# Loading the second expert of each pair through the scalar engine's DMA queue

## The chip, the cores and the metric

The kernel runs on one core of a Trainium2 chip. The core has a matmul engine (TensorE, PE in the profile, with its weight loads shown apart as PEld), a vector engine (DVE), a scalar engine (ACT), GpSimd (POOL) and a sync engine (SP) that computes nothing and only issues DMA transfers. All transfers run on the same 16 DMA engines; a transfer is put on the queue of the engine that issues it. The metric is the device time of one execution in microseconds. The figure for a kernel is the median over several runs.

## The reference: what is computed

Two transformer blocks over 256 tokens of width 1024, everything in fp32, batch 1. The first block mixes (a spatial gating unit and attention), then has an MLP of width 4096 and a gated projection. The second has a state-space and attention mixer and ends in a mixture of experts, which is the part that matters here:

```python
t = h.reshape(-1, d)                       # 256 tokens x 1024
g_sel = argmax(t @ w_router_group)         # 1 group of 8
top_logit, top_local = top_k(in_group, 2)  # 2 experts of the 8 in that group
# for each of the 64 experts e, on the tokens that chose it:
hid = silu(xb @ w_gate[e]) * (xb @ w_up[e])    # 1024 -> 512
y   = hid @ w_down[e]                          # 512 -> 1024, times the token's gate, added up
```

There are 64 experts. Each has three matrices of 1024 x 512 fp32 (gate, up, down), 2 MB each, so the weights of the experts are 64 x 3 x 2 MB. Each token uses two experts, so an expert sees few tokens, and one that no token chose need not be loaded.

## The kernel before

The program is written engine by engine: each engine has its own instruction list, and semaphores order them. A semaphore is named after what it counts: `gated`, `upped` and `downed` count the pairs whose gate, up and down matmuls are done; `pair_landed[...]` counts landed weights.

**The first 700 us** (both mixers, the MLP) stream 1 MB weight panels through three raw buffers. The change doesn't touch them.

**The experts.** The 64 experts are taken in 32 pairs; two pairs make a couple. `experts(couple, odd, ...)` exists once for PE, once for ACT and once for DVE, and each handles pair `i = 2 * couple + odd`. PE's steps for a pair:

1. gate matmuls (line 1132, 32 matmuls), reading both experts' gate panels, then `gated` goes up
2. up matmuls (also line 1132, 32 matmuls), then `upped` goes up
3. small work: in odd pairs the gather of the next couple's tokens (L1102), in both the scatter of the pair before (L1112), and two turns (transposes, L1146 and L1150)
4. down matmuls (L1168, 32 matmuls), then `downed` goes up

Before each of the three big steps PE waits for the weights of both experts, e = 0 and e = 1:

```python
for e in range(2):
    pe.wait_ge(pair_landed["down", e], 16 * (i + 1))
```

ACT's steps for a pair: silu of the gate result after `gated` (L722), a copy of the turned hidden values (L726), a sum over the gates (L730), and after `downed` a scaled copy of both halves of the result (L736). In odd pairs it also copies gathered tokens (L716).

**Buffers.** Up and down have one buffer for each of e = 0 and 1; gate has two, for even pairs in the tile `slots` and for odd pairs in the tile `areas`. So gate of pair i + 2 can be loaded once gate of pair i has been used, but up and down of pair i + 1 only when those of pair i have been used.

**Loading.** SP issues all the loads, one instruction of 2 MB for each expert and matrix (L376). After the first pair (and gate of pair 1) its fixed order is up(i), gate(i+1), down(i), up(i+1), ..., each time e = 0 and then e = 1. Each step first reads the two token counts from `count_i` (L380), then waits until the buffer was used, and issues the loads with a condition: an expert with zero tokens is not moved, though its semaphore is still counted up. SP works strictly in this order, so gate(i+1) is issued behind up(i) even where its buffer came free earlier. A second pass over all experts, for experts with over 64 tokens, is in the program but is not entered with these inputs.

Of the kernel before, what the change touches and what calls it, by code (L numbers as in the profile page):

```python
# [26 lines left out]
P = 128  # L27
D = 1024
S = 256
# [13 lines left out]
SLOTS = 64  # L43
PAIRS = NE // 2
# [44 lines left out]
def program(nc, x_in, p_in, norm_mix_g, w_in, w_sgu, b_sgu, ln_v_g, ln_v_b, rel_bias, w_out, norm_ffn_g,  # L89
# [24 lines left out]
    with ExitStack() as ctx:  # L114
        def sb(name, shape, dt=F32):
            return ctx.enter_context(nc.sbuf_tensor(name, shape, dt))
# [51 lines left out]
        count_i = sb("count_i", [P, NE + 1], I32)  # L168
# [154 lines left out]
        @block.sync  # L323
        def _(sp):
            sp.dma_start(x[:, :, :], x_in[0].rearrange("(m p) c -> p m c", p=P)).then_inc(x_loaded, 16)
            def load_rows():
                sources = {"norm_mix_g": norm_mix_g, "norm_ffn_g": norm_ffn_g, "norm_ple_g": norm_ple_g, "b_sgu": b_sgu,
                           "norm_mix_2": norm_mix_2, "conv_w": conv_w, "conv_b": conv_b, "ssd_norm": ssd_norm,
                           "attn_norm": attn_norm, "norm_ffn_2": norm_ffn_2}
                for name, (first, n) in ROWS.items():  # L330
                    src = sources[name]
                    if name == "conv_w":
                        src = src[0].rearrange("j (c p) -> (j c) p", p=P)
                    elif name == "b_sgu":
                        src = src[0]
                    else:
                        src = src[0].rearrange("(c p) -> c p", p=P)
                    sp.dma_start(small_rows[first:first + n], src).then_inc(rows_loaded, 16)

            for q in range(2 * NP):  # L340
                p, (kind, j) = q // 2, PANELS[q // 2]
                k = shape(p)[0] // 2
                if q >= RAW:
                    sp.wait_ge(w_ready, q - RAW + 1)
                sp.dma_start(loaded(q),
                             panel_source(kind, j)[:, k * (q % 2):k * (q % 2) + k, :]).then_inc(landed[q % RAW], 16)
                if q == 0:
                    load_rows()
                if q == 1:
                    sp.dma_start(table[0:BUCKETS, :], rel_bias).then_inc(table_loaded, 16)  # L350
                    sp.dma_start(area(6)[0:BUCKETS + 1, 0:LINE], bucket_of_line).then_inc(bucket_loaded, 16)
                    sp.dma_start(w_s, w_sgu[0].rearrange("g t s -> t g s")).then_inc(ws_loaded, 16)
                if q == 3:
                    sp.dma_start(ln_vecs[:, 0, :], ln_v_g.to_broadcast([P, D])).then_inc(ln_loaded, 16)
                    sp.dma_start(ln_vecs[:, 1, :], ln_v_b.to_broadcast([P, D])).then_inc(ln_loaded, 16)
                if q == 11:
                    for n, v in enumerate((dt_bias, a_log, d_skip, attn_sinks)):
                        sp.dma_start(heads4[:, n, :], v.to_broadcast([P, HEADS])).then_inc(heads_loaded, 16)
                    sp.dma_start(dtw[:, :, :], columns(w_in_2, 2560, HEADS)).then_inc(dtw_loaded, 16)


            def load(w, i, pair, odd, beyond):
                weights, used = {"gate": (w_gate, gated), "up": (w_up, upped), "down": (w_down, downed)}[w]


                tokens = [None if beyond is None else tokens_of(pair, e) for e in range(2)]
                if isinstance(i, int) and i == 0:
                    sp.wait_ge(panel_done, NP)
                elif isinstance(i, int) and w == "gate":
                    sp.wait_ge(t_made, MT)  # L370
                    sp.wait_ge(routed, 1)
                else:
                    sp.wait_ge(used, i - 1 if w == "gate" else i)
                for e in range(2):
                    cond = {} if beyond is None else {"cond": tokens[e] > beyond}
                    sp.dma_start(expert_panel(w, e, odd), weights[0, 2 * pair + e].rearrange("(p k) n -> p k n", p=P),  # L376
                                 **cond).then_inc(pair_landed["odd_gate" if w == "gate" and odd else w, e], 16)

            def tokens_of(pair, e):
                return sp.value_load(count_i[0:1, bass.ds(2 * pair + e, 1)], min_val=0, max_val=S)  # L380

            def rest_of_pass(first, beyond):

                with sp.Fori(0, PAIRS // 2 - 1) as j:
                    for n in (1, 2):
                        for w, ahead in (("up", 0), ("gate", 1), ("down", 0)):
                            load(w, 2 * j + n + ahead + first, 2 * j + n + ahead, (n + ahead) % 2, beyond)
                for w in ("up", "down"):
                    load(w, first + PAIRS - 1, PAIRS - 1, 1, beyond)

            for w in ("gate", "up", "down"):
                load(w, 0, 0, 0, None)
            load("gate", 1, 1, 1, None)
            sp.wait_ge(marks_done, 1)
            fullest = sp.value_load(count_i[0:1, NE:NE + 1], min_val=0, max_val=S)
            rest_of_pass(0, 0)
            with sp.If(fullest > SLOTS):
                with sp.Fori(1, PASSES) as r:
                    for w in ("gate", "up", "down"):
                        load(w, r * PAIRS, 0, 0, r * SLOTS)  # L400
                    load("gate", r * PAIRS + 1, 1, 1, r * SLOTS)
                    rest_of_pass(r * PAIRS, r * SLOTS)
            for m in range(MT):
                sp.wait_ge(out_ready, m + 1)
                sp.dma_start(out[0, P * m:P * m + P, :], xn[:, m, :]).then_inc(out_stored, 16)
            sp.wait_ge(out_stored, 16 * MT)
# [61 lines left out]
        def _(act):  # L468
# [244 lines left out]
            def gather(couple, half):  # L713

                act.wait_ge(gathered, 4 * couple + 2 * half + 1)
                act_(xeT[:, 4 * half:4 * half + 2].rearrange("p k o s -> p (k o s)"), banks[0][:, :], ACT.Copy).then_inc(xe_a, 1)  # L716

            def experts(couple, odd, first=False, last=False):

                i = 2 * couple + odd  # L720
                act.wait_ge(gated, i + 1)
                act_(h_e[:, :], banks[2][:, :], ACT.Silu).then_inc(silu_ready, 1)  # L722
                if odd and not last:
                    gather(couple + 1, 0)
                act.wait_ge(he_turned, i + 1)
                act_(heT[:, :, :].rearrange("p c s -> p (c s)"), banks[2][:, :], ACT.Copy).then_inc(heT_ready, 1)  # L726
                act.wait_ge(put_turned, i + 1)
                if not first:
                    act.wait_ge(ye_d, i)
                act_(gates_seen[:, :], banks[3][:, 0:S], ACT.Copy, accum_out=gate_of_slot).then_inc(gate_kept, 1)  # L730
                if odd and not last:
                    gather(couple + 1, 1)
                act.wait_ge(gate_kept, i + 1)
                act.wait_ge(downed, i + 1)
                for half in range(2):
                    act_(y_hi[:, 512 * half:512 * half + 512], banks[half][:, :], ACT.Copy, scale=gate_of_slot).then_inc(ye_a, 1)  # L736

            gather(0, 0)
            gather(0, 1)
            experts(0, 0, first=True)  # L740
            experts(0, 1)
            fullest = act.value_load(count_i[0:1, NE:NE + 1], min_val=0, max_val=S)
            with act.Fori(1, PAIRS // 2 - 1) as j:
                experts(j, 0)
                experts(j, 1)
            experts(PAIRS // 2 - 1, 0)
            experts(PAIRS // 2 - 1, 1, last=True)
            with act.If(fullest > SLOTS):
                with act.Fori(1, PASSES) as r:
                    gather(r * (PAIRS // 2), 0)  # L750
                    gather(r * (PAIRS // 2), 1)
                    with act.Fori(0, PAIRS // 2 - 1) as j:
                        experts(r * (PAIRS // 2) + j, 0)
                        experts(r * (PAIRS // 2) + j, 1)
                    experts(r * (PAIRS // 2) + (PAIRS // 2 - 1), 0)
                    experts(r * (PAIRS // 2) + (PAIRS // 2 - 1), 1, last=True)
            load_roots()
            act.wait_ge(x_ready, X_MOE)
            sum_squares(x, D, xn)
# [1041 lines left out]
```

## Time and profile before

| | |
|---|---|
| runs (3): median, lowest, highest | 1677.53, 1676.45, 1678.44 us |
| profiled execution: its own time | 1678.98 us |
| its span, first to last instruction | 1677.2 us |
| PE busy | 1508.0 us, 90% |
| DVE, ACT busy | 577.1 us (34%), 452.3 us (27%) |
| moved by DMA | 489.21 MB, mean 292 GB/s |
| queues: SP's (hardware) and GpSimd's (software) | 484.17 MB and 4.26 MB |

The span is the stretch that the trace shows; the time of the same execution is 1.8 us longer. The page cuts the span into 40 slices of 41.9 us; experts run from slice 18 on (about 717 us) to the end. A busy PE in this profile need not be PE at its peak. "SPq" and "ACTq" are instructions that an engine's sequencer handles itself, such as the issue of a transfer.

### The profile page before, as it was taken

What the parts mean: (1) busy time and instruction counts of PE and PEld (TensorE: products, weight loads), DVE (VectorE), ACT (ScalarE), POOL (GpSimd) and SP (SyncE); (2) the same over time, 40 slices, a digit from 0 to 9 for tenths busy, and PEclk for the clock granted to TensorE, in tenths of its full rate; (3) what the DMA queues carried; (4) which work ended last, traced back from release to release, by engine and by line L of the source; (5) the groups of instructions that cost most, each with busy time, mean ns of one, the idle gap of its engine ahead of it and who ended that gap; (6) DMA issues with size and microseconds to landing.
All of it is one profiled execution on the core that took longest, in us unless ns stands there. A gap on an engine that the chain in (4) does not pass through costs nothing.

```text
span 1677.2 us, 20152 instructions
## 1 busy us (share of the span) xinstructions
PE 1508.0 (90%) x7961; PEld 959.4 (57%) x7963; DVE 577.1 (34%) x934; ACT 452.3 (27%) x720; POOL 25.9 (2%) x34
## 2 busy tenths in 40 slices
PE   7999979999979988959999889888988989999976
PEld 5897869988769977744344334434433443444432
DVE  5745655644554897541111011111101111111102
ACT  5435645543444464321011011111101111111101
POOL 1000000000000000020000000000000000000000
PEclk9999989999979997979999999999999999999998
DMA  8463344455333331287999999999999999998993
GB/s 291 157 236 113 122 147 149 162 193 188 135 119 120 105 121 68 57 368 308 404 389 428 429 428 429 428 429 428 429 427 429 428 429 395 416 428 370 429 408 127
DMA packets 80269, 489.21 MB, mean 292 GB/s; under 512 B 6423, under 2 KB 8595, under 8 KB 56788
## 3 DMA queue, kind: packets, MB, share of 16 engines
q1 hardware_dynamic: 79028, 484.17, 71.3%
q0 software_dynamic: 1184, 4.26, 0.8%
q8 instruction: 39, 0.64, 0.2%
q14 instruction: 18, 0.15, 0.0%
HBM read 506.20 MB, written 1.08 MB: 302 GB/s over the span
## 4 chain that ended last, share of the span: by engine, by line
PE 54%; DMA 20%; DVE 7%; issue 2%; ACT 2%; SPq 1%; DVEq 0%; ACTq 0%
DMA slots<-in_w_down_dram 20%; PE bank L796 19%; PE bank L1168 15%; PE bank L1132 12%; PE bank L1102 3%; PE bank L1112 2%; DVE w_lo L1267 1%; SPq L376 1%; DVE h_lo L1257 1%; PE bank L779 1%; DVE areas L1517 1%; PE bank L1053 1%; DVE xeT L1701 1%; PE bank L1043 0%; DVE areas L1220 0%
## 5 line engine op out<-in xcount | busy, mean ns | idle before, releaser
L1132 PE MATMUL bank<-slots,xeT 128*64 128x512 f32 x1536 | 335.4, 592 | 0.8 <-issue 0.8
L1168 PE MATMUL bank<-slots,heT 128*64 128x512 f32 x1024 | 250.1, 645 | 65.5 <-DMA slots<-in_w_down_dram 64.0
L1132 PEld LDWEIGHTS bank<-slots,xeT 128*64 128x64 f32 x1536 | 118.7, 137 | 211.2 <-issue 211.2
L1267 DVE TENSOR_TENSOR w_lo<-raw,w_hi 128x2048 fp32r<-128x2048 f32 (+2 forms) x98 | 208.9, 2166 | 75.6 <-ACT w_hi L522 75.4
L1168 PEld LDWEIGHTS bank<-slots,heT 128*64 128x64 f32 x1024 | 82.6, 148 | 214.6 <-issue 211.5
L522 ACT ACTIVATE w_hi<-raw 128x2048 fp32r<-128x2048 f32 (+2 forms) x98 | 173.6, 1816 | 62.1 <-PE bank L796 56.6
L796 PE MATMUL bank<-h_hi,w_hi 128*128 128x256 f32 x560 | 160.8, 287 | 0.2 <-DVE h_lo L1257 0.2
L796 PE MATMUL bank<-h_lo,w_hi 128*128 128x256 f32 x560 | 159.1, 284 | 0.0
L796 PE MATMUL bank<-h_hi,w_lo 128*128 128x256 f32 x560 | 159.1, 284 | 0.0
L1723 DVE SCALAR_TENSOR_TENSOR y_lo<-bank,stats,y_hi 128x512 fp32r<-128x512 f32 x64 | 45.1, 746 | 313.1 <-ACT y_hi L736 313.1
L1710 DVE TENSOR_TENSOR h_e<-bank,h_e 128x512 f32<-128x512 f32 x32 | 22.1, 692 | 363.7 <-PE bank L1132 363.7
L796 PE MATMUL bank<-w_hi,h_hi 128*128 128x512 f32 (+1 forms) x344 | 138.1, 402 | 7.9 <-DVE h_lo L1257 3.0
L796 PE MATMUL bank<-w_hi,h_lo 128*128 128x512 f32 (+1 forms) x344 | 134.1, 390 | 0.0
L796 PE MATMUL bank<-w_lo,h_hi 128*128 128x512 f32 (+1 forms) x344 | 133.9, 389 | 0.0
L736 ACT ACTIVATE y_hi<-bank,stats 128x512 fp32r<-128x512 f32 x64 | 40.5, 684 | 339.1 <-PE bank L1168 339.1
L1132 PE MATMUL bank<-areas,xeT 128*64 128x512 f32 x512 | 112.8, 592 | 0.0
L796 PEld LDWEIGHTS bank<-h_hi,w_hi 128*128 128x128 f32 x560 | 108.2, 193 | 2.1 <-issue 0.6
L796 PEld LDWEIGHTS bank<-h_lo,w_hi 128*128 128x128 f32 x560 | 108.2, 193 | 0.0
L796 PEld LDWEIGHTS bank<-h_hi,w_lo 128*128 128x128 f32 x560 | 108.1, 193 | 0.0
L1132 PEld LDWEIGHTS bank<-areas,xeT 128*64 128x64 f32 x512 | 40.3, 137 | 69.6 <-issue 69.6
L796 PEld LDWEIGHTS bank<-w_hi,h_hi 128*128 128x128 f32 x344 | 66.0, 192 | 24.5 <-issue 7.2
L796 PEld LDWEIGHTS bank<-w_hi,h_lo 128*128 128x128 f32 x344 | 65.6, 191 | 13.8
(301 smaller groups left out, 1637.5 us busy)
## 6 DMA issues: line engine op xcount, KB each, us to landing
slots<-in_w_up_dram SPq DMA_DIRECT2D x64, 2048.0 KB, 15.4
slots<-in_w_down_dram SPq DMA_DIRECT2D x64, 2048.0 KB, 19.3
slots<-in_w_gate_dram SPq DMA_DIRECT2D x32, 2048.0 KB, 19.3
areas<-in_w_gate_dram SPq DMA_DIRECT2D x32, 2048.0 KB, 21.8
raw<-in_w_in_dram SPq DMA_DIRECT2D x42, 1024.0 KB, 6.2
raw<-in_w_ff_dram SPq DMA_DIRECT2D x32, 1024.0 KB, 5.3
raw<-in_w_out_dram SPq DMA_DIRECT2D x12, 1024.0 KB, 5.1
raw<-in_w_ple_gate_dram SPq DMA_DIRECT2D x4, 1024.0 KB, 5.6
```

The lines of the kernel that those rows point to most:

```text
L376: sp.dma_start(expert_panel(w, e, odd), weights[0, 2 * pair + e].rearrange("(p k) n -> p k n", p=P), **cond).then_inc(pair_landed["odd_gat ...
L522: last = act_(hi, source, ACT.Copy)
L736: act_(y_hi[:, 512 * half:512 * half + 512], banks[half][:, :], ACT.Copy, scale=gate_of_slot).then_inc(ye_a, 1)
L779: last = turn_tile(banks[b][:, at:at + P], src[:, m, P * k:P * k + P], ident[:, :])
L796: last = mm(psum, a[i][a_at], b[j][b_at], start=(start and n == 0), stop=(stop and n == 2))
L1102: last = mm(banks[b][:, S * (k % 2):S * (k % 2) + S], t[:, m, P * k:P * k + P], pick_r[:, m, :, :].rearrange("p e s -> p (e s)"), start=(m ...
L1112: last = mm(banks[4 + 2 * m + half][:, :], put[:, m, :], y[:, 512 * half:512 * half + 512], start=False, stop=False)
L1132: last = mm(bank[SLOTS * e:SLOTS * e + SLOTS, :], xeT[:, k, odd, SLOTS * e:SLOTS * e + SLOTS], expert_panel(w, e, odd)[:, k, :], start=(k ...
L1168: last = mm(banks[half][SLOTS * e:SLOTS * e + SLOTS, :], heT[:, c, SLOTS * e:SLOTS * e + SLOTS], expert_panel("down", e, odd)[:, c, 512 * ...
L1267: last = tt(lo, source, hi, ALU.subtract)
L1710: tt(h_e[:, :], banks[3][:, :], h_e[:, :], ALU.mult).then_inc(he_ready, 1)
L1723: last_part = stt(y_lo[:, 512 * half:512 * half + 512], banks[half][:, :], gate_of_slot, y_hi[:, 512 * half:512 * half + 512].bitcast(F32) ...
```

## The change

From pair 1's up on (and gate from pair 2 on), SP issues only the load of e = 0. The load of e = 1 is issued by ACT, through ACT's own DMA queue, by a new function `load_second` that ACT calls at three places of its `experts`: gate of pair i + 2 behind the silu of pair i, up of pair i + 1 after the gates' sum (in odd pairs after the second token copy too), and down of pair i + 1 behind the two scaled copies of pair i. No new semaphore wait is added there, as ACT has already waited for what shows the buffer to be free. What is read, its sizes, buffers and conditions stay. PE's and DVE's programs stay as they are.

```diff
-            def load(w, i, pair, odd, beyond):
+            def load(w, i, pair, odd, beyond, both=True):
...
-                for e in range(2):
+                for e in range(2 if both else 1):
...
                         for w, ahead in (("up", 0), ("gate", 1), ("down", 0)):
-                            load(w, 2 * j + n + ahead + first, 2 * j + n + ahead, (n + ahead) % 2, beyond)
+                            load(w, 2 * j + n + ahead + first, 2 * j + n + ahead, (n + ahead) % 2, beyond, both=False)
...
+            def load_second(w, pair, odd, beyond):
+
+                weights = {"gate": w_gate, "up": w_up, "down": w_down}[w]
+                tokens = act.value_load(count_i[0:1, bass.ds(2 * pair + 1, 1)], min_val=0, max_val=S)
+                act.dma_start(expert_panel(w, 1, odd), weights[0, 2 * pair + 1].rearrange("(p k) n -> p k n", p=P),
+                              cond=tokens > beyond).then_inc(pair_landed["odd_gate" if w == "gate" and odd else w, 1], 16)
+
-            def experts(couple, odd, first=False, last=False):
+            def experts(couple, odd, in_pass, beyond, first=False, last=False):
...
                 act.wait_ge(gated, i + 1)
                 act_(h_e[:, :], banks[2][:, :], ACT.Silu).then_inc(silu_ready, 1)
+                if not last:
+                    load_second("gate", 2 * in_pass + odd + 2, odd, beyond)
                 if odd and not last:
                     gather(couple + 1, 0)
...
                 if odd and not last:
                     gather(couple + 1, 1)
+                if not (odd and last):
+                    load_second("up", 2 * in_pass + odd + 1, 1 - odd, beyond)
                 act.wait_ge(gate_kept, i + 1)
                 act.wait_ge(downed, i + 1)
                 for half in range(2):
                     act_(y_hi[:, 512 * half:512 * half + 512], banks[half][:, :], ACT.Copy, scale=gate_of_slot).then_inc(ye_a, 1)
+                if not (odd and last):
+                    load_second("down", 2 * in_pass + odd + 1, 1 - odd, beyond)
```

Where the instructions stand: ACT's program of one even pair in the loop over couples, before (`h_e` is the silu, `heT` the turned copy, `gates_seen` the gates' sum, `y_hi` the scaled copies).

```order
L722 ACTIVATE h_e<-bank 128x512 [waits gated]
L726 ACTIVATE heT<-bank 128x512 [waits he_turned]
L730 ACTIVATE gates_seen,stats<-bank 128x256 [waits ye_by_vector,put_turned]
L736 ACTIVATE y_hi<-bank,stats 128x512 [waits downed,gate_kept]
L736 ACTIVATE y_hi<-bank,stats 128x512
```

The first and the last part of the same pair in the changed kernel (the up load, left out here, stands between them in the same way; "ISA" rows are register work).

```order
L729 ACTIVATE h_e<-bank 128x512 [waits gated]
L721 ISA
L721 TENSOR_LOAD count_i
L721 ISA x2
L722 ISA
L722 DMA slots<-in_w_gate_dram 128x4096
L735 ACTIVATE heT<-bank 128x512 [waits he_turned]
...
L747 ACTIVATE y_hi<-bank,stats 128x512 [waits downed,gate_kept]
L747 ACTIVATE y_hi<-bank,stats 128x512
L721 TENSOR_LOAD count_i
L721 ISA x2
L722 ISA
L722 DMA slots<-in_w_down_dram 128x4096
```

Three loads of e = 1 have moved into ACT's program, each behind work of ACT and with no wait of its own.

SP's program at up and gate in the same loop, as before:

```order
L376 ISA [waits upped]
L376 DMA slots<-in_w_up_dram 128x4096
L376 ISA
L376 DMA slots<-in_w_up_dram 128x4096
...
L376 ISA [waits gated]
L376 DMA slots<-in_w_gate_dram 128x4096
L376 ISA
L376 DMA slots<-in_w_gate_dram 128x4096
```

And in the changed kernel:

```order
L376 ISA [waits upped]
L376 DMA slots<-in_w_up_dram 128x4096
...
L376 ISA [waits gated]
L376 DMA slots<-in_w_gate_dram 128x4096
```

SP still takes up before gate, with one load each; the gate load of e = 1 no longer stands behind SP's wait for `upped`.

## Rows read from the trace of the kernel before

**Rows 1.** The page: slices of the span, and queues.
```profile
DMA  8463344455333331287999999999999999998993
GB/s 291 157 236 113 122 147 149 162 193 188 135 119 120 105 121 68 57 368 308 404 389 428 429 428 429 428 429 428 429 427 429 428 429 395 416 428 370 429 408 127
...
q1 hardware_dynamic: 79028, 484.17, 71.3%
q0 software_dynamic: 1184, 4.26, 0.8%
```

**Rows 2.** Waits over the whole span: us in total, times, longest us.
```profile
ACT y_hi L736 <- PE bank L1168: 339.1, 32, 15.3
...
ACT h_e L722 <- PE bank L1132: 178.7, 32, 7.0
ACT heT L726 <- PE bank L1146: 160.3, 32, 8.8
...
PE bank L1168 <- DMA slots<-in_w_down_dram: 64.0, 17, 6.6
```

**Rows 3.** Stretches: us, engines' busy time (instructions), TensorE clock, DMA share, GB/s.
```profile
758.00:770.00 12.00, 11.01 (x54) 4.51 (x50) 0.69 (x1) 0.92 (x2) 0.00 (x0) 1.00 0.11 27
823.00:827.00 4.00, 3.69 (x20) 2.30 (x16) 0.69 (x1) 0.49 (x1) 0.00 (x0) 1.00 0.62 184
845.00:851.00 6.00, 5.83 (x37) 3.43 (x33) 1.38 (x2) 0.99 (x2) 0.00 (x0) 1.00 0.41 137
1422.00:1427.00 5.00, 5.00 (x31) 2.96 (x28) 0.69 (x1) 0.60 (x1) 0.00 (x0) 1.00 0.37 102
1509.00:1513.00 4.00, 3.53 (x20) 2.43 (x18) 0.69 (x1) 0.86 (x3) 0.00 (x0) 1.00 0.73 246
1531.00:1536.00 5.00, 5.00 (x34) 3.05 (x31) 0.94 (x2) 0.60 (x1) 0.00 (x0) 1.00 0.36 95
1633.00:1637.00 4.00, 4.00 (x22) 1.47 (x20) 0.86 (x2) 1.27 (x2) 0.00 (x0) 1.00 0.38 94
851.00:1422.00 571.00, 523.36 (x2486) 229.65 (x2488) 74.89 (x118) 67.47 (x139) 0.00 (x0) 0.96 1.01 428
```

**Rows 4.** Timeline at one gap of pair 23: start us, length us, what.
```profile
1417.91 7.07 PE L1132 MATMUL bank<-slots,xeT 128*64 128x512 f32 x32
1418.15 0.60 ACT L722 ACTIVATE h_e<-bank 128x512 f32<-128x512 f32 x1 [5.54 <-PE bank L1132]
...
1425.29 0.97 SPq L376 DMA_DIRECT2D slots<-in_w_up_dram  x2
```

**Rows 5.** Timeline at the first gap, pair 0, and the next PE wait.
```profile
754.09 13.95 PE L1132 MATMUL bank<-slots,xeT 128*64 128x512 f32 x64 [0.83 <-issue]
...
768.38 1.02 SPq L376 DMA_DIRECT2D slots<-in_w_up_dram  x2
...
801.80 8.42 PE L1168 MATMUL bank<-slots,heT 128*64 128x512 f32 x32 [3.69 <-DMA slots<-in_w_down_dram]
```

**Rows 6.** Stretches at the end of the first gap, columns as above.
```profile
768.50:769.00 0.50, 0.10 (x1) 0.11 (x2) 0.34 (x1) 0.00 (x0) 0.00 (x0) 1.00 0.00 0
769.00:769.50 0.50, 0.50 (x5) 0.50 (x6) 0.00 (x0) 0.00 (x0) 0.00 (x0) 1.00 1.50 328
```

**Rows 7.** SP's loads (L376, L380): duration ns min/median/max.
```profile
L380 SPq TENSOR_LOAD <-count_i x184: 261/268/283, 746.8 to 1618.3; - x184
...
L376 SPq FUSED_REGOPS  x184: 149/174/200, 768.1 to 1635.9; - x184
L376 SPq DMA_DIRECT2D slots<-in_w_up_dram x64: 88/333/532, 718.2 to 1617.4; - x64
```

**Rows 8.** Timeline of the last two pairs.
```profile
1603.16 1.00 SPq L376 DMA_DIRECT2D slots<-in_w_down_dram  x2
...
1625.85 9.40 PE L1168 MATMUL bank<-slots,heT 128*64 128x512 f32 x32 [6.61 <-DMA slots<-in_w_down_dram]
...
1652.65 7.09 PE L1168 MATMUL bank<-slots,heT 128*64 128x512 f32 x32
```

More of the change, by code:

```diff
@@ L386, in rest_of_pass @@
                         for w, ahead in (("up", 0), ("gate", 1), ("down", 0)):
-                            load(w, 2 * j + n + ahead + first, 2 * j + n + ahead, (n + ahead) % 2, beyond)
+                            load(w, 2 * j + n + ahead + first, 2 * j + n + ahead, (n + ahead) % 2, beyond, both=False)
                 for w in ("up", "down"):
-                    load(w, first + PAIRS - 1, PAIRS - 1, 1, beyond)
+                    load(w, first + PAIRS - 1, PAIRS - 1, 1, beyond, both=False)
             for w in ("gate", "up", "down"):
@@ L736, in experts @@
                     act_(y_hi[:, 512 * half:512 * half + 512], banks[half][:, :], ACT.Copy, scale=gate_of_slot).then_inc(ye_a, 1)
+                if not (odd and last):
+                    load_second("down", 2 * in_pass + odd + 1, 1 - odd, beyond)
             gather(0, 0)
             gather(0, 1)
-            experts(0, 0, first=True)
-            experts(0, 1)
+            act.wait_ge(marks_done, 1)
+            experts(0, 0, 0, 0, first=True)
+            experts(0, 1, 0, 0)
             fullest = act.value_load(count_i[0:1, NE:NE + 1], min_val=0, max_val=S)
             with act.Fori(1, PAIRS // 2 - 1) as j:
[L744 to L747, printed above, removed]
+                experts(j, 0, j, 0)
+                experts(j, 1, j, 0)
+            experts(PAIRS // 2 - 1, 0, PAIRS // 2 - 1, 0, last=True)
+            experts(PAIRS // 2 - 1, 1, PAIRS // 2 - 1, 0, last=True)
             with act.If(fullest > SLOTS):
@@ L752, in _ @@
                     with act.Fori(0, PAIRS // 2 - 1) as j:
[L753 to L756, printed above, removed]
+                        experts(r * (PAIRS // 2) + j, 0, j, r * SLOTS)
+                        experts(r * (PAIRS // 2) + j, 1, j, r * SLOTS)
+                    experts(r * (PAIRS // 2) + (PAIRS // 2 - 1), 0, PAIRS // 2 - 1, r * SLOTS, last=True)
+                    experts(r * (PAIRS // 2) + (PAIRS // 2 - 1), 1, PAIRS // 2 - 1, r * SLOTS, last=True)
             load_roots()
```

## The prediction

> **What bounds the kernel now.** I read the page's slices first. In the part with the experts the DMA row shows 9 (90% or more) in nearly every slice and the GB/s row stands at 427 to 429 for a dozen slices in a row [rows 1]. That is a flat ceiling: from 851 to 1422 us the DMA share is 1.01 at 428 GB/s [rows 3]. One expert matrix is 2 MB = 2.097 million bytes, so a load takes 2.097/428 = 4.9 us and the six of a pair 29.4 us. PE, when it need not wait, is faster: in these 571 us it was busy 523 [rows 3], although part of that was at the lower of its two clock levels. The table of waits says the same from PE's side: PE waited 64.0 us in 17 pieces, each time for the down weights [rows 2]. So the bound is transfer time, and its end can move in only two ways: the bytes move at another rate, or the DMA engines stand idle for less time. The change leaves the bytes alone.
>
> So the question is where the DMA engines stand idle. I looked through the stretch in windows of 10 us and then narrowed them. There are seven gaps, and idle time is width times (1 - share) [rows 3]: 758 to 770: 12 x 0.89 = 10.7; 823 to 827: 1.5; 845 to 851: 3.5; 1422 to 1427: 3.2; 1509 to 1513: 1.1; 1531 to 1536: 3.2; 1633 to 1637: 2.5 us. The first six sum to 23.2 us. The last is of another kind: it stands before the very last load pair (down of pair 31), for which nothing else could be moved.
>
> Who ends a gap is seen in the timeline. In the gap at 1422 all buffers are full except one: gate of pair 23 has been used (PE goes over to the up matmuls at 1417.91), so gate of pair 25 could be loaded. But SP stands at its wait for `upped` and issues up at 1425.29, and gate only after that [rows 4]. The first gap has the same form: PE begins gate of pair 0 at 754.09, gate and up take 13.95 us together, and SP's first issue is at 768.38 [rows 5]; gate of pair 0 was used halfway, at about 761.
>
> **What the change does to a gap.** ACT issues gate(i+2) of e = 1 right behind the silu, without regard to `upped`. When does its first byte move? The silu starts 0.24 us after PE's gate step ended and takes 0.60 [rows 4]. Then come a token load (0.27), register work (two of about 0.17) and the issue itself (0.33); I take SP's figures [rows 7], since the trace has no issue by ACT. That is 0.24 + 0.60 + 0.27 + 0.34 + 0.33 = 1.8 us if nothing of it overlaps. From issue to moving data takes about 0.9 us: issued at 768.38, none in the half microsecond from 768.5, moving in that from 769.0 [rows 5, 6]. So the load fills the DMA engines from about gated + 2.7 to gated + 7.6 us. SP's up load starts at gated + 6.9 (the up step's length, from 7.07 less the overlap) + 0.5 (1417.91 + 6.9 to 1425.29) + 0.9 = gated + 8.3 [rows 4]. So a gap that lies ahead of an up issue can be filled by up to 4.9 us, with up to about 1 us left at its end.
>
> **The sum.** Upper end: each of the six gaps is filled wholly but for the cap of 4.9 in the first: 4.9 + 1.5 + 3.5 + 3.2 + 1.1 + 3.2 = 17.4 us. Lower end: 1 us stays in each of the other five: 4.9 + 0.5 + 2.5 + 2.2 + 0.1 + 2.2 = 12.4 us. Does the gain reach the end? PE follows the DMA engines: behind every gap but the last there is a wait of PE for down, behind the first at 801.80 (3.69 us) [rows 5], and in the last stretch at 1625.85 (6.61 us) [rows 8]. That last one is 6.61 us, more than the last gap alone gives back. From there the end is PE's own work, which the change doesn't touch. One term comes on top. After that 6.61 us wait the down step takes 9.40 us, against 7.09 us one pair later [rows 8]; it shows the lower clock after idling. If the wait is cut to a small rest, up to 2.3 us are saved. I take about half, since I can't say how much wait is left: 1.1 us. Middle of 12.4 and 17.4 is 14.9, and I round the total down to 15, because a DMA queue that is ahead finds its buffers full a little sooner in the next gap.
>
> **What it costs.** SP loses one issue a step (0.5 us a load with its register work [rows 7]) and gains nothing by it. ACT gets three loads a pair, 1.0 us each. They are covered: ACT idles 178.7/32 = 5.6 us before each silu, 5.0 us before each turned copy and 10.6 us before the scaled copies [rows 2], and each load stands ahead of one of those waits. If an issue by ACT took 5 us and more, the cover would be gone and PE would wait for ACT's copies; the trace shows SP issuing at 0.33 us each, 0.53 at most, also with three or four loads still outstanding [rows 7], so I cost it at zero. The e = 1 loads of up and down are issued later than before: down by the copies and the issue (about 2 us), up by the small step of PE (3 to 6 us). While the DMA engines are saturated they have other loads to move then, so this costs nothing in total; the wait only moves, partly from down to up, since gate(i+2) of e = 1 now stands ahead of up(i+1) in ACT's queue.
>
> The unknown is the rate with two hardware queues at work at once. The trace has GpSimd's queue with 4.26 MB only [rows 1] and no stretch with two full queues. Below, nothing excludes a gain: the share of 1.01 says that there is no room inside a stretch, so I bound the gain by zero. Above, each 1% of rate is 9 us of the 900 us of transfers. The nearest rows are the ones at 427 GB/s against 429 [rows 1], 0.5% or 4 us. I take no change.
>
> The Trainium skill bears on this, in "DMA: Bandwidth & Descriptors", section "Rules for kernel authors": spreading transfers over several issuing engines doesn't help bandwidth, as all run on the same 16 DMA engines and interleave; it only saves issue time. The flat 428 GB/s agrees with that, and by this rule alone the sum would be 0 us. My sum doesn't need more bandwidth: it rests on one load being issued some 5.5 us earlier, into idle time. The same page, section "Queues, rings and completion order", says that each DMA engine takes turns between the queues that have work; no stretch of this trace has two full ones, so it can't confirm it.
>
> The profiled execution is 1678.98 us, so 1664.0; it stands 1.45 us above the median of the runs shown, 1677.53, which gives 1662.5.
>
> **The rivals.**
> *No change (1677.5).* The bytes and the rate are the same, and but for 26 us (the seven gaps) of some 930 the DMA engines are saturated. For it: PE could be ahead of nothing, and a filled gap could come back as a longer one at the next place where buffers are full. Against it: between the third and the fourth gap lie 571 us with PE waits, in which a lead of 3.5 us can't be lost [rows 3]. Only the skill's rule, read as "issuing from two engines gives nothing", points here.
>
> *Half the gain (about 1670).* Gate of e = 1 gets ahead of up of e = 1, while ACT's up load comes 3 to 6 us late. PE then waits for up, the release of up's buffers is late too, and new small gaps form. If 1 to 2 us more stay in each of five gaps, 5 to 10 us of the 15 are gone: 1667 to 1672.
>
> *Slower (about 1685).* Two full queues alternating on each DMA engine lower the rate. Break-even is 15/900 = 1.7%, that is 421 GB/s in the saturated stretch; slower by over 0.2% needs (15 + 3.4)/900 = 2.0%, that is 419. At 417 (2.6% lower) the loads take 23 us more: 1677.5 - 15 + 23 = 1685. For it: nothing in the rows but that it is untried. Against it: loads of 2 MB in long pieces, and the engines' rate stays at 427 to 429 whatever buffer and matrix is loaded [rows 1].
>
> **How the numbers follow.** Forecast (12 to 18 us less): 0.60. Half the gain (4 to 12 less): 0.16. No change: 0.11. Slower through the rate: 0.10. More than 18 us less: 0.03. Over 0.2% (3.4 us, about what a measurement of this kernel can tell from no change) faster is then 0.79, within it 0.11, slower 0.10. The range runs from 1657 (the upper end of the sum, 17.4, and the whole clock term, 2.3, with 1 us of rate) to 1677: it takes in half the gain and the better part of no change, and leaves out 3 + 4 + 10 = 17 in 100. The forecast's own range is 1659 to 1666.
>
> **What the profile of the changed kernel would show.** A third DMA queue with about 190 MB. The saturated stretch still at 428. The gaps at the steps of pairs 0, 2, 3, 23, 26 and 27 down to about 1 us each, the first to about 6. ACT's issues right behind the silu, ACT's own waits shorter by the 1 us of each load and PE's waits for ACT unchanged. PE's waits for down shorter and some small ones for up. What would make it wrong: a saturated rate of 421 or less; issues by ACT that take several us; gaps of the old length in new places.

## The result and the profile after

| | median, us (lowest to highest, runs) |
|---|---|
| before | 1677.99 (1676.45 to 1678.70, 4) |
| changed | 1666.09 (1661.56 to 1667.91, 4) |
| ratio | 0.9929, 95% interval 0.9912 to 0.9946 |

The change makes the kernel 0.7% faster, 11.9 us. Run again later (last run below) it gave 0.9934 (0.9921 to 0.9946). The forecast was 15 us, 1662.5 with a range of 1657 to 1677. One line of the change stands outside the part shown ahead: ACT now also waits once for `marks_done`, which says that the token counts are ready, before it takes up the first pair.

The page of the changed kernel, with the rows that answer to [rows 1]: slices of the DMA engines' busy share and rate, and the queues (packets, MB, share of 16 engines).

```profile
span 1666.2 us, 20460 instructions
...
DMA  8463343555334322278999999999999999999993
GB/s 294 157 235 117 113 145 130 188 189 184 132 114 139 102 101 72 88 296 358 417 409 429 428 429 428 428 428 430 428 428 428 428 429 419 405 429 394 429 419 129
...
q1 hardware_dynamic: 65780, 291.22, 44.7%
q10 hardware_dynamic: 13248, 192.94, 27.4%
q0 software_dynamic: 1184, 4.26, 0.8%
```

ACT's queue q10 is new and carries 193 MB. The plateau is the same, 428 to 430 GB/s. Two hardware queues at once neither raised nor lowered the rate. Among the experts' slices those with gaps have changed: near the end 395, 416 and 370 GB/s before, now 419, 405 and 394 (a slice is 41.7 us now).

The gaps, as in [rows 3] (us, engines' busy time, TensorE clock, DMA share, GB/s):

```profile
760.00:772.00 12.00, 11.15 (x54) 4.53 (x50) 0.69 (x1) 1.97 (x3) 0.00 (x0) 1.00 0.59 205
825.00:829.00 4.00, 3.53 (x18) 1.20 (x18) 0.42 (x1) 0.90 (x3) 0.00 (x0) 1.00 0.96 348
847.00:849.00 2.00, 2.00 (x19) 2.00 (x18) 0.64 (x2) 0.60 (x1) 0.00 (x0) 1.00 0.80 229
848.00:1417.00 569.00, 522.67 (x2487) 233.48 (x2487) 75.63 (x119) 68.28 (x140) 0.00 (x0) 0.96 1.01 427
1417.00:1425.00 8.00, 8.00 (x48) 4.05 (x45) 0.92 (x2) 0.60 (x1) 0.00 (x0) 1.00 0.90 317
1523.00:1531.00 8.00, 8.00 (x47) 4.37 (x43) 0.94 (x2) 0.60 (x1) 0.00 (x0) 1.00 0.90 320
1623.00:1626.00 3.00, 3.00 (x16) 1.21 (x14) 1.05 (x2) 1.27 (x2) 0.00 (x0) 1.00 0.71 213
```

The first gap fell by share from 10.7 to 12 x 0.41 = 4.9 us, by bytes from 12 x (1 - 27/428) = 11.2 to 6.3 us. The others are nearly gone by share: 0.8 us in each of the windows from 1417 and 1523, where there were 3.2 us. By bytes they are not: 8 us at 317 GB/s lack 8 x (1 - 317/428) = 2.1 us of transfers. An equally long stretch of the kernel before, around its gap at 1422, lacks 8 x (1 - 201/428) = 4.2:

```profile
1420.00:1428.00 8.00, 7.83 (x47) 4.44 (x43) 1.38 (x2) 0.98 (x2) 0.00 (x0) 1.00 0.56 201
```

So half of it is left. Share and rate part where a load starts: half a microsecond of [rows 6] has a share of 1.50 at only 328 GB/s. That makes short gaps look shorter by share.

How a gap is filled shows at pair 23, in the timeline of ACT's and then of SP's issues (answers to [rows 4]):

```profile
1415.82 0.60 ACT L729 ACTIVATE h_e<-bank 128x512 f32<-128x512 f32 x1 [5.53 <-PE bank L1146]
1416.75 0.34 ACTq L722 DMA_DIRECT2D areas<-in_w_gate_dram  x1
...
1427.66 0.35 ACTq L722 DMA_DIRECT2D slots<-in_w_up_dram  x1
```
```profile
1422.96 0.33 SPq L376 DMA_DIRECT2D slots<-in_w_up_dram  x1
1424.95 0.33 SPq L376 DMA_DIRECT2D areas<-in_w_gate_dram  x1
```

ACT issues gate of e = 1 at 1416.75, 6.2 us ahead of SP's up, 0.93 us after the silu began. And it issues up of e = 1 at 1427.66, 4.7 us after SP's up of e = 0, where before both went out together.

ACT's wait before the silu and PE's waits for weights, which answer to [rows 2] (us in total, times, longest):

```profile
ACT h_e L729 <- PE bank L1146: 171.6, 31, 5.5
...
PE bank L1182 <- DMA slots<-in_w_down_dram: 40.9, 14, 4.6
PE bank L1146 <- DMA slots<-in_w_up_dram: 11.5, 12, 1.8
```

The wait for down fell from 64.0 to 40.9 us and a new wait for up of 11.5 us has come. The last pairs, which answer to [rows 8]:

```profile
1616.97 7.09 PE L1182 MATMUL bank<-slots,heT 128*64 128x512 f32 x32 [2.46 <-DMA slots<-in_w_down_dram]
```

The last wait is 2.46 us (it was 6.61) and the down step behind it takes 7.09 us, no longer 9.40: in this profile the whole clock term of 2.3 us was saved (the granted clock was 0.75 in the step of 9.40 us and is 1.00 in this one). It isn't always: in the profile of the changed kernel run again the same step has about the same wait before it and takes 8.63 us.

```profile
1615.50 8.63 PE L1182 MATMUL bank<-slots,heT 128*64 128x512 f32 x32 [2.40 <-DMA slots<-in_w_down_dram]
```

**Where the two profiles differ outside the experts.** PE's first gate matmul starts at 754.09 us before [rows 5] and at 756.32 after. In the profiles of the eleven runs below it starts anywhere between 751.8 and 756.6, whatever was changed, so 2.2 us of this pair of profiles belong to the first part. From the first gate matmul to the end it is 1677.2 - 754.09 = 923.1 us before and 1666.2 - 756.32 = 909.9 after: 13.2 us less.

### The profile page after: what moved, and what is told of

Its sections match the earlier page's. It is cut to its first block, busy times and chain, and to the rows that moved or that the text cites. A ratio compares the mean times of both kernels' runs of the same rounds, so it can differ in the third digit from the quotient of the medians.

```text
span 1666.2 us, 20460 instructions
## 1 busy us (share of the span) xinstructions
PE 1505.2 (90%) x7961; PEld 961.4 (58%) x7963; DVE 577.6 (35%) x934; ACT 452.4 (27%) x721; POOL 25.9 (2%) x34
## 4 chain that ended last, share of the span: by engine, by line
PE 57%; DMA 19%; DVE 7%; ACT 2%; issue 2%; SPq 0%; DVEq 0%; ACTq 0%
PE bank L810 20%; DMA slots<-in_w_down_dram 18%; PE bank L1146 14%; PE bank L1182 14%; PE bank L1116 3%; PE bank L1126 2%; DVE w_lo L1281 1%; DMA slots<-in_w_up_dram 1%; PE bank L793 1%; DVE areas L1531 1%; DVE h_lo L1271 1%; PE bank L1067 1%; DVE xeT L1715 0%; PE bank L1057 0%; DVE areas L1234 0%
## 5 line engine op out<-in xcount | busy, mean ns | idle before, releaser
L1146 PE MATMUL bank<-slots,xeT 128*64 128x512 f32 x1536 | 337.6, 593 | 12.3 <-DMA slots<-in_w_up_dram 11.5
L1182 PE MATMUL bank<-slots,heT 128*64 128x512 f32 x1024 | 243.1, 630 | 44.3 <-DMA slots<-in_w_down_dram 40.9
L1146 PEld LDWEIGHTS bank<-slots,xeT 128*64 128x64 f32 x1536 | 122.6, 137 | 221.9 <-issue 221.9
## 6 DMA issues: line engine op xcount, KB each, us to landing
slots<-in_w_down_dram ACTq DMA_DIRECT2D x31, 2048.0 KB, 15.1
```

Of the source, the lines that this page charges most:

```text
L1146: last = mm(bank[SLOTS * e:SLOTS * e + SLOTS, :], xeT[:, k, odd, SLOTS * e:SLOTS * e + SLOTS], expert_panel(w, e, odd)[:, k, :], start=(k ...
L1182: last = mm(banks[half][SLOTS * e:SLOTS * e + SLOTS, :], heT[:, c, SLOTS * e:SLOTS * e + SLOTS], expert_panel("down", e, odd)[:, c, 512 * ...
```

## The experiments

The ledger that I use for all runs: time from the first gate matmul to the end of the span, and how many microseconds of transfers the DMA engines miss, by bytes, in the first 100 us from that matmul (A: the first gap and those around the first empty expert), in the next 520 us (B: the saturated part) and in the next 230 us (C: the gaps around the two other empty experts). Missing time is length x (1 - GB/s / 428); for the kernels before and after it comes from these stretches:

```profile
754.09:854.09 100.00, 94.17 (x461) 41.34 (x462) 13.76 (x22) 12.57 (x27) 0.00 (x0) 0.98 0.84 350
854.09:1374.09 520.00, 473.25 (x2236) 205.59 (x2235) 67.02 (x106) 59.46 (x121) 0.00 (x0) 0.95 1.01 429
1374.09:1604.09 230.00, 220.29 (x1087) 101.53 (x1087) 33.43 (x53) 30.78 (x63) 0.00 (x0) 0.99 0.97 410
```
```profile
756.32:856.32 100.00, 96.81 (x478) 42.52 (x480) 14.54 (x23) 13.71 (x27) 0.00 (x0) 1.00 0.94 386
856.32:1376.32 520.00, 474.32 (x2252) 212.69 (x2247) 67.23 (x106) 61.61 (x126) 0.00 (x0) 0.96 1.01 428
1376.32:1606.32 230.00, 222.11 (x1087) 96.84 (x1087) 33.40 (x53) 29.25 (x59) 0.00 (x0) 1.00 0.99 416
```

| kernel | ratio to before (95%) | median - before, us | gate to end | A | B | C |
|---|---|---|---|---|---|---|
| before | | | 923.1 | 18.2 | 0 | 9.7 |
| changed | 0.9929 (0.9912, 0.9946) | -11.9 | 909.9 | 9.8 | 0 | 6.4 |
| changed, again | 0.9934 (0.9921, 0.9946) | -9.5 | 913.5 | 10.3 | 0 | 9.1 |
| gate alone on ACT | 0.9970 (0.9958, 0.9982) | -3.5 | 920.6 | 15.2 | 0 | 10.2 |
| gate and down on ACT | 0.9953 (0.9941, 0.9965) | -6.9 | 916.4 | 10.3 | 1.2 | 10.7 |
| up and down on ACT | 1.0027 (1.0017, 1.0037) | +4.7 | 927.0 | 19.2 | 0 | 11.3 |
| up, then gate, on ACT | 1.0074 (1.0058, 1.0091) | +13.7 | 934.0 | 22.4 | 1.2 | 13.4 |
| gate late on ACT | 1.1113 (1.1093, 1.1133) | +186.2 | 1099.6 | 22.2 | 104.5 | 42.5 |
| SP alone, both gates first | 0.9923 (0.9909, 0.9936) | -11.7 | 908.0 | 6.8 | 0 | 7.5 |
| SP alone, split order | 0.9893 (0.9875, 0.9912) | -17.8 | 902.8 | 8.2 | 0 | 0.5 |
| SP alone, first pair both | 0.9918 (0.9905, 0.9931) | -12.6 | 906.3 | 8.6 | 0 | 3.2 |

(One GB/s in the rate is 0.2 us in A, 1.2 in B, 0.5 in C; 429 GB/s counts as nothing missing. The ratio need not be that of the two medians, so it can differ a little from the column beside it: 0.9934 of the kernel before would be 11 us less, where the medians say 9.5.)

The last four columns come from one profile of each kernel. How far such a profile can be trusted shows in the two of the changed kernel: A is 9.8 and 10.3, but C is 6.4 and 9.1, so differences of 3 us in C say little. The ledger closes all the same: in every row but "gate late" the change in A + B + C gives the change in the time from the first gate matmul to the end within 2 us. So the differences between these kernels are idle DMA time.

**Gate alone on ACT's queue.** ACT keeps `load_second("gate", ...)` only; SP loads both experts' up and down:

```diff
-    load(w, ..., beyond, both=False)
+    load(w, ..., beyond, both=w != "gate")
...
-    load_second("up", 2 * in_pass + odd + 1, 1 - odd, beyond)
-    load_second("down", 2 * in_pass + odd + 1, 1 - odd, beyond)
```

> Only the gate load of e = 1 is issued by ACT behind the silu; up and down of both experts stay with SP as before. Theory of the gaps (the gain is one load issued earlier, into idle DMA time): the whole gain of the change, 10 to 14 us under the kernel before, and the gaps ahead of up issues down to about 1 us. Rival theory of the two queues (the gain comes from loads that run side by side on two queues): one third of the loads of e = 1 is on ACT's queue, so 3 to 5 us.

Measured: 3.5 us faster, which is what the rival expected and not my theory. But its ledger doesn't fit the rival either: the first gap is filled as in the changed kernel, and a new one of 4 us comes behind it (from 806 to 810 us the rate is 143 GB/s). PE's first down wait in this kernel is as long as in the kernel before (3.69 us, [rows 5]):

```profile
800.07 10.09 PE L1178 MATMUL bank<-slots,heT 128*64 128x512 f32 x32 [3.75 <-DMA slots<-in_w_down_dram]
```

In the changed kernel PE has no wait for down at this place, only one of 1.04 us for up before it. Median times from issue to landing in this kernel, of the loads issued from 745 us on:

```profile
slots<-in_w_up_dram SPq DMA_DIRECT2D x62, 2048.0 KB, 15.3
slots<-in_w_down_dram SPq DMA_DIRECT2D x62, 2048.0 KB, 18.0
slots<-in_w_gate_dram ACTq DMA_DIRECT2D x15, 2048.0 KB, 13.6
slots<-in_w_gate_dram SPq DMA_DIRECT2D x15, 2048.0 KB, 18.9
```

The same kind of load lands after 13.6 us from ACT's queue and after 18.9 from SP's. A queue with little in it is served as well as the full one, so the gate load, needed last, can overtake the down loads that PE waits for. At the first down wait it did. The down load of e = 1 was issued at 776.6 on SP's queue and landed after 23.4 us, at 800.0; ACT's gate load was issued at 783.4 and landed after 15.4 us, at 798.7, before it:

```profile
L376 SPq DMA_DIRECT2D slots<-in_w_down_dram x1: 333/333/333, 776.6 to 776.6; - x1
DMA to landing us min/median/max: 23.4/23.4/23.4
```
```profile
L722 ACTq DMA_DIRECT2D areas<-in_w_gate_dram x1: 350/350/350, 783.4 to 783.4; - x1
DMA to landing us min/median/max: 15.4/15.4/15.4
```

That the overtaking accounts for all of the missing gain is an inference.

**Up and down on ACT's queue,** gate of both experts with SP (`both=w == "gate"`, and no `load_second("gate", ...)`).

> Up and down of e = 1 are issued by ACT, gate of both experts by SP behind its wait for upped, as before. Theory of the gaps: no load is issued earlier than before, so no gain: within 2 us of the kernel before, with gaps of 3 to 4 us ahead of the up issues as before. Two queues: 7 to 10 us faster.

Measured: 4.7 us slower, outside the 2 us expected. No gain, so working with two queues brings nothing by itself; and a real cost that I had set at zero. All gaps are there and a little longer (A 19.2, C 11.3). Two things could cause it, and no run separates them: ACT issues these loads later than SP did, and the two queues, unequally full, land them in another order.

**SP alone, both gate loads first.** The kernel before with two entries exchanged:

```diff
-    for w, ahead in (("up", 0), ("gate", 1), ("down", 0)):
+    for w, ahead in (("gate", 1), ("up", 0), ("down", 0)):
```

> The kernel before with SP's order changed from up, gate, down to gate, up, down, both experts by SP, ACT issues nothing. Theory of the gaps: both gate loads (9.8 us) are issued right after gated, so every gap but the first is filled with no rest and the first shrinks from 11 to about 4.5 us: 15 to 19 us under the kernel before, more than the change itself. Two queues: no gain, within 2 us, as all loads are on one queue; or slower, since gate of pair i+2 now stands ahead of up of pair i+1 and PE waits for up.

Measured: 11.7 us faster, as much as the change, with one queue and nothing for ACT to do. So the second queue is not needed for the gain. It is less than the 15 to 19 expected: A is down to 6.8 us, but PE now waits for up, where it had waited for down (one wait of 1.0 us for down is left):

```profile
PE bank L1132 <- DMA slots<-in_w_up_dram: 44.5, 12, 5.1
```

Two gate loads ahead of up (9.8 us) are more than the later gaps hold, and the rest delays up. From the first gate matmul to the end this kernel gains 15.1 us in its profile, so part of the shortfall may be scatter of the first part.

**Gate late on ACT.** In the changed kernel, `load_second("gate", ...)` is moved from behind the silu to behind the copy of the turned hidden values, just ahead of up's.

> The changed kernel with one thing moved: ACT issues the gate load of e = 1 behind its copy of the turned hidden values, that is after upped, not behind the silu. All three loads of e = 1 stay on ACT's queue. Theory of the gaps: the gain is gone, within 2 us of the kernel before, gaps of 3 to 4 us come back ahead of the up issues. Two queues: still 11 to 13 us under the kernel before.

Measured: 186 us slower. Both theories failed. ACT's issues, PE's steps and the DMA engines in one pair of this kernel:

```profile
1005.24 0.34 ACTq L722 DMA_DIRECT2D areas<-in_w_gate_dram  x1
1006.68 0.35 ACTq L722 DMA_DIRECT2D slots<-in_w_up_dram  x1
```
```profile
1028.29 8.40 PE L1146 MATMUL bank<-slots,xeT 128*64 128x512 f32 x32 [5.77 <-DMA slots<-in_w_up_dram]
```
```profile
1034.00:1039.00 5.00, 5.00 (x26) 2.76 (x23) 0.69 (x1) 0.00 (x0) 0.00 (x0) 1.00 0.25 52
```

Gate of pair i + 2 now stands right ahead of up of pair i + 1, with no 7 us between them. The two queues share the DMA engines equally in this stretch, as the bytes moved from 1008 to 1028 us show:

```profile
q1 hardware_dynamic: 297, 4.34, 50.7%
q10 hardware_dynamic: 295, 4.31, 50.3%
```

Two loads behind each other on a queue that gets half the rate are 2 x 2 x 4.9 = 20 us, and PE begins up 21.6 us after its issue. SP's issue at 1015.97 is followed by none until 1037.03, so the DMA engines run dry (share 0.25) until PE has finished up and SP issues again. That repeats in 27 of the 32 pairs: 201.2 us of waits for up in 27 pieces.

**Up, then gate, on ACT.** To test that explanation, the two loads are exchanged: `load_second("gate", ...)` directly behind `load_second("up", ...)`, both still after `upped`.

> The changed kernel with ACT's gate load moved behind its up load, so the order on ACT's queue is up, gate, down, all after upped. Theory (the 186 us of the run with the gate load just ahead of the up load came from up standing behind gate on one queue, not from ACT or from two queues): that loss is gone, the time is near the kernel before, 0 to 8 us above it, and PE's waits for up are small. If instead issuing gate late from ACT is what costs: still over 50 us slower.

Measured: 13.7 us slower. The 186 us are gone with the exchange of two neighbouring loads, so they came from the order on the queue. The size was missed (0 to 8 expected): gate and up of e = 1 now both go out later than in the kernel before, and every gap grows (A 22.4, C 13.4).

**All experts loaded.** In the kernel before and in the changed one the condition of the first pass is made always true, so that the three empty experts are moved too:

```diff
-    cond = {} if beyond is None else {"cond": tokens[e] > beyond}
+    cond = {} if beyond is None else {"cond": tokens[e] > (beyond if not isinstance(beyond, int) else -1)}
```

> The kernel before, loading also the three experts that no token chose (nine loads more, 44 us of transfers). Theory of the gaps: all gaps but the first and the last are due to the loads left out, so they vanish here; PE had waited elsewhere, so the time rises by about 44 less the vanished gaps of 13 us, that is 28 to 34 us above the kernel before.

> The changed kernel, loading also the three experts that no token chose. Theory of the gaps: only the first gap is left to be filled, so it is 3 to 7 us under the kernel before that loads all experts (4.9 us of the first gap, and some of the clock). If the gain were spread over all pairs (two queues, or SP's shorter steps), it would still be 11 us or more.

Measured: 1705.81 us (28.9 above the kernel before, within the 28 to 34 expected, ratio 1.0164, 1.0143 to 1.0186) and 1697.87 us (1.0123, 1.0102 to 1.0145), so the change is worth 7.9 us here, as against 11.9: just above the 3 to 7 expected, and under the 11 of the rival. C is zero in both, A is 11.4 and 6.8 us: what is left in A is the first gap, 4.6 us shorter. So the gaps behind the empty experts are due to those, and the change gains in them only if they exist. The gain is 3.3 us more than the first gap gives; PE's waits for weights fell by 7 to 11 us in total (81.0 for down, to 57.7 for down, 12.3 for up and one of 4.3 before a down step that the trace puts down to nothing), and how much of the rest is clock and how much scatter I didn't separate.

**SP alone, split order.** If only the order counts, the changed kernel's order on SP's queue should do:

```diff
-    for w, ahead in (("up", 0), ("gate", 1), ("down", 0)):
+    for w, ahead, which in (("gate", 1, (1,)), ("up", 0, (0, 1)), ("gate", 1, (0,)), ("down", 0, (0, 1))):
```

where `which` says for which experts of the pair the step issues loads.

> SP issues everything, ACT nothing, in the order in which the changed kernel's loads become ready: gate of pair i+2 for e = 1 (behind gated), up of both experts (behind upped), gate for e = 0, down of both. If the gain of the change is the order alone: 11 to 14 us under the kernel before, with the time of the changed kernel. If the second queue has a share in it: clearly less, under 8 us. Against the run with both gate loads first, fewer and shorter waits of PE for up.

Measured: 17.8 us faster than before, 1659.11 us, the best of all. More than expected: it beats the changed kernel. The stretches B and C of the ledger:

```profile
852.98:1372.98 520.00, 477.67 (x2270) 209.16 (x2268) 68.69 (x108) 61.55 (x126) 0.00 (x0) 0.96 1.01 429
1372.98:1602.98 230.00, 224.02 (x1100) 95.47 (x1096) 33.06 (x52) 30.18 (x62) 0.00 (x0) 1.00 1.01 427
```

C has gone from 9.7 to 0.5 us; in the changed kernel 6.4 and 9.1 are left. SP issues its gate load of e = 1 0.5 us after PE's gate step (ACT 1.2 us, 1416.75 above less the end of the gate step at 1415.6), and up and down of e = 1 are as early as before.

**Gate and down on ACT,** up of both experts with SP.

> Gate and down of e = 1 on ACT's queue, up of both experts with SP. Theory (the run with gate alone on ACT's queue gained only 3.5 us because its gate load had an empty queue and overtook the down loads that PE waits for): with down of e = 1 ahead of gate on the same queue, the overtaking is half gone and the gain comes back, 9 to 14 us under the kernel before, first gap about 7 us, and no new gap of 4 us at pair 1. If not the overtaking but the share of loads on ACT's queue decides: between the two, 5 to 8 us.

Measured: 6.9 us faster, the value of the rival. The gap of 4 us at pair 1 has gone as expected (A 10.3), yet C is 10.7. With two, four and six of ACT's loads per couple the gains are 3.5, 6.9 and 11.9 us. That fits unequal queues being served equally, but it doesn't show it, and four of ACT's loads without the early gate load cost 4.7 us. The cause of the rest in C I didn't follow up.

**SP alone, both gate loads first for the first pair only,** as only the first gap is longer than one load.

> The order on SP alone (gate e = 1, up, gate e = 0, down), but with both gate loads ahead of up for the first pair only, where the gap is 11 us long and one load fills only 4.9 of it. Theory: about 2 us less idle in the first gap (7 to 5 us), the rest as in the run with the split order, so 18 to 21 us under the kernel before. If PE's first up wait takes it back: no better than the split order, 17 to 18 us.

Measured: 12.6 us faster, 5 us less than the split order, each against its own runs of the kernel before (from first gate to end 906.3 against 902.8 us), and under both expectations. The 2 us expected did not come: A is 8.6 us against 8.2, what the first gap gave up came back at the next ones, and C is 3.2 against 0.5.

**The changed kernel again.**

> The changed kernel itself, again, on the same chip as the two others of this call: 10 to 14 us under the kernel before. In its profile the time from the first gate matmul to the end should again be about 910 us, while the first part may differ by some 2 us to either side.

Measured: 9.5 us by the medians, ratio 0.9934 (0.9921 to 0.9946), by the medians just under the 10 to 14 expected, and 913.5 us from first gate to end, not 910. The changed kernel scatters more than the one before in these runs: 1661.6 to 1667.9 us within one set.

## Why the prediction came out

**The bound and the mechanism were right.** Transfers are the bound, the plateau is unchanged, and the gain comes from loads issued about 6 us earlier into idle DMA time. Shown three ways: the order alone on one queue gives it (split order, -17.8), the two queues without the earlier gate load don't (+4.7), and without empty experts the part behind them is gone (C is zero). What is shown cleanly holds for one queue. With two queues the same early load gave 3.5, 6.9 or 11.9 us, as other loads went with it to ACT's queue or not; why is argued above and not shown.

**The size was off: 11.9 us against 15, and 9.5 the second time.** Both lie in what the prediction called half the gain (4 to 12 us less, chance 0.16), just outside its forecast of 12 to 18; that the time of 1666.1 lies well inside the stated range owes much to that range's width. The terms that failed:
- *"Up to about 1 us left"* in each later gap. By bytes about 2 us are left (2.1 at 1417 to 1425, 2.0 at 1523 to 1531), and C fell by 3.3 us only, 9.7 to 6.4, and by 0.6 when run again, where the sum has 4.5 to 7.5 us for these three gaps. So most of the gain lies in A, which fell by 8.4 and 7.9 us against 7.9 to 9.9 in the sum. I had measured the gaps by share, which hides the ramp of a load.
- *"The e = 1 loads of up and down are issued later ..., so this costs nothing in total."* It costs 4.7 us when done alone, of which A and C show 2.6. The argument holds in the saturated part (B is 0); that it fails next to the gaps because there are no other loads to move is my reading, no run singles it out.
- The clock term: taken at 1.1. In the profile it was 2.3 us, in the other direction, but only 9.40 - 8.63 = 0.8 when run again, behind a wait of 2.40 us where the first profile has 2.46. That the first profile has the whole of it is luck.

The first gap gave the 4.9 us of the forecast (11.2 to 6.3 by bytes).

**ACT's costs were hidden** as forecast. ACT's issue takes 0.34 us, and it still idles before each silu, at most 5.5 us at a time but for the first of 8.3. The sign that ACT's own waits would be shorter by the 1 us of each load did not come: they are 171.6 + 8.3 us before the silu (178.7 before), since the issues are not counted as busy time. The token load and the register work ran beside the silu: the issue began 0.93 us after the silu's start, where my terms gave 0.60 + 0.27 + 0.34 = 1.2.

**The rivals.** No change is refuted. The lower rate too: 427 to 430 GB/s with two queues. This agrees with the rule of the Trainium skill ("DMA: Bandwidth & Descriptors", section "Rules for kernel authors") that several issuing engines don't add bandwidth; the gain needs none. "Half the gain" has its mechanism in the trace, PE's new waits for up of 11.5 us and 1 us more left in a gap than forecast, and by its size the result belongs to it as much as to the forecast; the run with the late gate load shows what it can cost.

## What to carry to other kernels

In a kernel that is bound by transfers, look for the idle gaps of the DMA engines, by bytes and not by share, and for the issue that ends each; a load whose buffer has been free for microseconds and that waits behind another wait of its issuer is worth moving ahead by itself. Try that by reordering the issuer first: a few lines on SP gave 17.8 us, the second queue 11.9 and 9.5. Splitting a stream over two queues changes the order in which loads land, since both are served alike, so what PE needs last should not sit right ahead of what it needs next (186 us here), nor, as far as the two runs with fewer loads on ACT tell, alone in the short queue.

## What the runs showed that I had not expected

- Exchanging two neighbouring loads on ACT's queue (gate before up, both after `upped`) moved the time from +13.7 to +186.2 us. A loop of buffers can settle at a slower period, here one with the DMA engines dry for part of each pair (342 GB/s in the 520 us of B).
- Issue to landing depends on the queue's own backlog: gate loads took 13.6 us from ACT's nearly empty queue and 18.9 us from SP's in the same kernel. That is as the Trainium skill has it ("DMA: Bandwidth & Descriptors", section "Queues, rings and completion order"): each DMA engine takes turns between the queues that have work. The trace agrees: 4.34 and 4.31 MB from the two queues in 20 us in which both had loads.
- The start of the experts' part varied between 751.8 and 756.6 us over the profiles, though nothing before it was changed.
